# Head norms summed with tokens on partitions, and the state inputs of an S5 layer regrouped

## The reference, cut to what matters

```
x = concat(meta_tokens, x); h = rms_norm(x, norm_pre[0])
q, k, v, gate_a, u, gate_b = split(h @ w_in)          # 8 query heads, 2 key heads of 128
q = rope(rms_norm(q per head, q_norm)); k = rope(rms_norm(k per head, k_norm))
y_a = attention(q, k, v) * silu(gate_a)
# S5, in each of two directions, 64 groups of 16 channels, 64 complex states each:
bu = einsum('blgp,gnp->blgn', u, b_bar); s_t = a_bar * s_(t-1) + bu_t
y_b = glu(gelu(u * d_skip + sum over directions of Re(c . s))) * silu(gate_b)
h = concat(y_a, y_b) @ w_out
```

## Time and profile before

| | us |
|---|---|
| median of 3 runs | 2744.39 |
| lowest, highest | 2741.42, 2744.92 |
| the profiled execution, its own time | 2744.17 |
| its span, first to last instruction | 2742.2 |
| PE busy | 2499.8 (91%) |
| DVE, ACT, POOL busy | 1396.9, 1012.3, 1120.3 |
| mean granted TensorE clock | 0.966 |

### The profile page before, as it was taken

How to read it: one execution, slowest core, us unless ns; L and a number is a source line. 1 busy time by engine, 2 the same in 40 slices (tenths; PEclk the granted TensorE clock), 3 DMA queues, 4 the chain that set the end, 5 groups by cost and what they waited for, 6 DMA issues and landing times. The chain is left out here.

```text
span 2742.2 us, 40562 instructions
## 1 busy us (share of the span) xinstructions
PE 2499.8 (91%) x15206; PEld 2161.4 (79%) x15206; DVE 1396.9 (51%) x2104; ACT 1012.3 (37%) x2146; POOL 1120.3 (41%) x1114
## 2 busy tenths in 40 slices
PE   6999998789998749899799999899898799999798
PEld 6988887678886648777588888787777689999687
DVE  6559886667775125414455443555655442222314
ACT  5232222767664331233233223355565420000331
POOL 3445542077774224411145454443343255554320
PEclk9999999999999979999899999999999899999999
DMA  7424443201103663535424333452434264442544
GB/s 168 111 67 151 140 132 127 99 21 48 48 33 115 155 163 116 174 132 163 117 76 149 129 123 128 149 168 101 165 120 155 74 233 163 140 140 94 189 164 153
DMA packets 271015, 349.27 MB, mean 127 GB/s; under 512 B 45652, under 2 KB 212206, under 8 KB 268406
## 3 DMA queue, kind: packets, MB, share of 16 engines
q1 hardware_dynamic: 226326, 268.32, 31.1%
q10 hardware_dynamic: 44512, 78.53, 8.2%
HBM read 223.23 MB, written 114.03 MB: 123 GB/s over the span
## 5 line engine op out<-in xcount | busy, mean ns | idle before, releaser
L1074 POOL TENSOR_TENSOR w_hi<-w_raw,ones 128x512 fp32r<-128x512 f32 (+1 forms) x232 | 287.3, 1238 | 753.1 <-PE r L1085 326.4
L1085 PE MATMUL r<-h_lo,w_hi 128*128 128x264 f32 (+1 forms) x1200 | 395.2, 329 | 7.4 <-PEq L2508 7.4
L1085 PE MATMUL r<-h_hi,w_lo 128*128 128x264 f32 (+1 forms) x1200 | 386.8, 322 | 0.0
L1085 PE MATMUL r<-h_hi,w_hi 128*128 128x264 f32 (+1 forms) x1200 | 386.0, 322 | 0.0
L1076 POOL TENSOR_TENSOR w_lo<-w_raw,w_hi 128x512 fp32r<-128x512 f32 (+1 forms) x232 | 355.7, 1533 | 18.2
L1085 PEld LDWEIGHTS r<-h_lo,w_hi 128*128 128x128 f32 x1200 | 226.7, 189 | 28.9 <-issue 9.9
L1085 PEld LDWEIGHTS r<-h_hi,w_hi 128*128 128x128 f32 x1200 | 226.8, 189 | 21.3 <-issue 2.4
L1085 PEld LDWEIGHTS r<-h_hi,w_lo 128*128 128x128 f32 x1200 | 226.7, 189 | 17.6
L1813 PE MATMUL o<-v,prob 116*116 116x129 f32 (+1 forms) x1296 | 166.1, 274 | 0.3 <-ACT prob L1863 0.3
L1085 PE MATMUL x<-h_lo,w_hi 128*128 128x264 f32 (+1 forms) x432 | 155.4, 360 | 7.0 <-POOL w_lo L1076 7.0
L1813 PEld LDWEIGHTS o<-v,prob 116*116 116x116 f32 (+1 forms) x1296 | 158.4, 180 | 3.9 <-ACT prob L1863 0.5
(11 more groups left out here) (383 smaller groups left out, 6294.2 us busy)
## 6 DMA issues: line engine op xcount, KB each, us to landing
w_raw<-in_w_in_even SPq DMA_DIRECT2D x72, 256.0 KB, 3.4
w_raw<-in_w_in_odd SPq DMA_DIRECT2D x64, 256.0 KB, 3.5
w_raw<-in_w_ogate SPq DMA_DIRECT2D x64, 256.0 KB, 2.8
v_d<-vs ACTq DMA_DIRECT2D x8, 1152.0 KB, 4.2
us<-u_d SPq DMA_DIRECT2D x16, 520.0 KB, 4.9
xc_d<-xc ACTq DMA_DIRECT2D x8, 1040.0 KB, 6.3
qk_d<-qk ACTq DMA_DIRECT2D x16, 520.0 KB, 2.7
qk<-qk_d SPq DMA_DIRECT2D x8, 1040.0 KB, 5.0
```

The costliest lines, as they stand in the source:

```text
L1074: self.nc.gpsimd.tensor_tensor(hi, raw, one, ALU.mult).then_inc(self.hi_done, 1)
L1085: ins = self.nc.tensor.matmul(bank[:, 0:n], w[:, u % self.buffers, k, :], z[:, off:off + n], start=(first and k == 0 and w is self.hi and ...
```

## The change

1. **Norm sums in front.** For each of the ten norms PE no longer multiplies ones (as weights) with `sq`. It takes slices of `sq` of 104 tokens as weights and one column of ones as the moving operand: ten matmuls, after step 2, each giving 104 sums in one PSUM column. ACT takes one root of 104x10, DVE one reciprocal of 104x10 (`inv`). PE then spreads them again, by ten transposes of a column of `inv` broadcast to 128, four after step 8, four after step 10, two after step 20. DVE multiplies `resn` with them in three parts, straight from PSUM. PE now waits for DVE's reciprocal (`found`) before step 9, and for the first of the three products (`scaled_by`) before the last two transposes. `turn_values` moves from steps 2, 4, 6 to 4, 6, 8.
2. **Six tables given.** `EARLY` goes from 2 to 6: 28 half tables are built after the gates of front instead of 20, and 12 of them are input tables. In s5_states SP loads six tables, for groups 0, 1, 2, 4, 5 and 7; DVE builds those of 3 and 6 there.
3. **State inputs.** The transposes are placed so that the real and imaginary part of one direction lie side by side as 128 weight columns; one matmul makes both. `w_in` has two buffers, and the transposes of group n + 1 go ahead of the sums of group n. The sums go to three PSUM slots of 1024 columns, each with one direction of four channel groups. ACT copies the forward direction to `Z`, DVE the backward one, each with 64 partitions by 4x130.

The diff, cut to its core:

```
-EARLY = 2
+EARLY = 6
...
+    NB, QUAD, SLOTS = G // GB, GB // 2, 3
+    MADE = [n for n in range(NB) if n not in STATES_GIVEN]
...
+            return t["Z"][side * NS:(side + 1) * NS, 1:CH + 1, q, g0:g0 + QUAD].rearrange("p c (b k) -> p b k c", b=2)
+
+        def sums(x, q):
+            return zb[x % SLOTS][q * NS:(q + 1) * NS, :].rearrange("p (b m) -> p b m", b=2)[:, :, 0:2 * CH].rearrange(
+                "p b (k c) -> p b k c", k=2)
+
...
+                        if i >= 2:
+                            sp.wait_ge(turned, 4 * (STATES_GIVEN[i - 2] + 1))
+                        sp.dma_start(given[:, i % 2].rearrange("p q g s f -> p (q g s f)"),
+                                     d["tab_in"][i].rearrange("p q h x -> p (q h x)")).then_inc(tab_loaded[i % 2], 16)
...
+                for n in range(NB):
+                    for h in range(2):
+                        r = 2 * n + h
+                        x = 4 * n + 2 * h + 1
+                        if r < 10:
+                            for k in range(0 if r == 0 else r + 2, r + 3):
+                                table_step(k // 6, k % 6)
+                        dve.wait_ge(summed, x + 1)
+                        for q in range(2):
+                            ins = v.tensor_copy(states(1, q, n, h), sums(x, q))
+                        ins.then_inc(back_out, 1)
...
-                        copied.wait(pe, nb, m - 1)
-                        for n in range(4):
...
-                    for g in range(GB):
-                        stored.wait(pe, nb, g - 3)
-                        for q in range(2):
-                            cols = slice(q * CH, (q + 1) * CH)
-                            nc.tensor.matmul(zp[g % 4][f, cols], wl[:, g, q, f], us[:, nb * GB + g, :],
-                                             start=True, stop=True)
-                            last = nc.tensor.matmul(zp[g % 4][r, cols], wl[:, g, q, r], us[:, nb * GB + g, ::-1],
-                                                    start=True, stop=True)
-                        last.then_inc(summed.sem, 1)
+                        if 4 * n + m >= 2:
...
+                            x = 4 * n + 2 * h + side
+                            if x >= SLOTS:
+                                y = x - SLOTS
+                                pe.wait_ge(back_out if y % 2 else ahead_out, y // 2 + 1)
+                            for k in range(QUAD):
+                                g = QUAD * h + k
+                                u = us[:, n * GB + g, ::-1] if side else us[:, n * GB + g, :]
+                                at = k // 2 * 512 + k % 2 * CH
+                                last = nc.tensor.matmul(zb[x % SLOTS][:, at:at + CH], wl[:, n % 2, g, side, :], u,
+                                                        start=True, stop=True)
+                            last.then_inc(summed, 1)
+
+                turn(0)
+                for n in range(NB):
+                    if n + 1 < NB:
+                        turn(n + 1)
+                    sum_up(n)
...
+                def keep(n):
+                    for m in range(4):
+                        act.wait_ge(turned, 4 * n + m + 1)
+                        if n >= 2:
+                            act.wait_ge(summed, 4 * (n - 1) - (2 if m < 2 else 0))
+                        nc.scalar.activation(wl[:, n % 2, 2 * m:2 * m + 2, :, :].rearrange("p g q m -> p (g q m)"),
+                                             tp[m % 2][:, :], ACT.Copy).then_inc(copied, 1)
+
+                keep(0)
+                for n in range(NB):
+                    if n + 1 < NB:
+                        keep(n + 1)
+                    for h in range(2):
+                        x = 4 * n + 2 * h
+                        act.wait_ge(summed, x + 1)
+                        for q in range(2):
+                            ins = nc.scalar.activation(states(0, q, n, h), sums(x, q), ACT.Copy)
+                        ins.then_inc(ahead_out, 1)
...
+    NORM_COLS, NORM_AT = L // 10, ((0, 4, 0), (4, 8, 1), (8, 10, 0))
...
-                    nc.tensor.matmul(bank[p % 2][:, 0:m], c["ones"][:, :], sq[:, off:off + m],
-                                     start=True, stop=True).then_inc(ss, 1)
...
+                    for i in range(10):
+                        last = nc.tensor.matmul(bank[0][0:NORM_COLS, i:i + 1], sq[:, i * NORM_COLS:(i + 1) * NORM_COLS],
+                                                c["ones"][:, 0:1], start=True, stop=True)
+                    last.then_inc(ss, 1)
...
+                    i0, i1, b = NORM_AT[part]
+                    if part == 0:
+                        pe.wait_ge(found, r + 1)
+                    elif part == 2:
+                        pe.wait_ge(scaled_by, 3 * r + 1)
+                    for i in range(i0, i1):
+                        at = (i - i0) * NORM_COLS
+                        last = nc.tensor.transpose(bank[b][:, at:at + NORM_COLS],
+                                                   inv[0:NORM_COLS, i:i + 1].broadcast_to([NORM_COLS, P]),
+                                                   c["ident"][0:NORM_COLS, 0:NORM_COLS])
+                    last.then_inc(spread, 1)
...
+                        if u - 1 in norm_at and n == 2:
+                            add_squares(norm_at[u - 1])
+                        if u - 1 in norm_at and n in (8, 10, 20):
+                            spread_norms(norm_at[u - 1], (8, 10, 20).index(n))
+                        if u - 1 in value_at and n in VALUE_STEPS:
+                            turn_values(value_at[u - 1], VALUE_STEPS.index(n))
...
+                    if r:
+                        act.wait_ge(spread, 3 * r)
+                    nc.scalar.activation(inv[0:NORM_COLS, :], bank[0][0:NORM_COLS, 0:10], ACT.Sqrt,
+                                         bias=c["eps"][0:NORM_COLS, :], scale=1.0 / HD).then_inc(root, 1)
 
                 def values_out(n, part):
...
+                    dve.wait_ge(root, r + 1)
+                    v.reciprocal(inv[0:NORM_COLS, :], inv[0:NORM_COLS, :]).then_inc(found, 1)
                     do(v.tensor_tensor(resn, qg, rope[:, 0, :], ALU.mult))
-                    for p, (off, m) in enumerate(PIECES):
-                        dve.wait_ge(root, NP * r + p + 1)
-                        ins = v.reciprocal(rs[:, off:off + m], rs[:, off:off + m])
-                        do(ins) if p == NP - 1 else do.free(ins)
                     dve.wait_ge(swapped, 64 * (r + 1))
-                    dve.wait_ge(ss, NP * (r + 1))
                     do(v.tensor_tensor(tm, qs, rope[:, 1, :], ALU.mult))
                     do(v.tensor_tensor(resn, resn, tm, ALU.add))
-                    do(v.tensor_tensor(resn, resn, rs, ALU.mult))
+                    for part, (i0, i1, b) in enumerate(NORM_AT):
+                        cols = slice(i0 * NORM_COLS, i1 * NORM_COLS)
+                        dve.wait_ge(spread, 3 * r + part + 1)
+                        v.tensor_tensor(resn[:, cols], resn[:, cols], bank[b][:, 0:(i1 - i0) * NORM_COLS],
+                                        ALU.mult).then_inc(scaled_by, 1)
+                    dve.wait_ge(scaled_by, 3 * (r + 1))
...
+                    if kind == "in":
+                        m = 2 * STATES_GIVEN[m // 2] + m % 2
```

More of the change, by code:

```diff
@@ L770, in _, with turn @@
             @block.tensor
             def _(pe):
-                turned.start(pe)
-                summed.start(pe)
-                f, r = slice(0, NS), slice(NS, P)
-                for nb in range(G // GB):
-                    b = nb % 2
-                    if nb < EARLY:
-                        pe.wait_ge(tab_loaded, 16 * (nb + 1))
-                    else:
-                        built.wait(pe, nb - EARLY, 1)
+                def turn(n):
+                    if n in MADE:
+                        pe.wait_ge(built, MADE.index(n) + 1)
+                    else:
+                        i = STATES_GIVEN.index(n)
+                        pe.wait_ge(tab_loaded[i % 2], 16 * (i // 2 + 1))
@@ L781, in _ @@
                     for m in range(4):
-                        copied.wait(pe, nb, m - 1)
-                        for n in range(4):
-                            g, q = 2 * m + n // 2, n % 2
-                            last = nc.tensor.transpose(tp[m % 2][:, n * P:(n + 1) * P],
-                                                       table[:, b, q, g].rearrange("p s q -> p (s q)"), c["ident"][:, :])
-                        last.then_inc(turned.sem, 1)
-                    copied.wait(pe, nb, 4)
@@ new lines, in turn, with sum_up @@
+                        for k in range(4):
+                            g, q = 2 * m + k // 2, k % 2
+                            last = nc.tensor.transpose(tp[m % 2][:, k // 2 * 256:k // 2 * 256 + 256].rearrange(
+                                "p (r q m) -> p r q m", r=2, q=2)[:, :, q, :],
+                                                       table(n)[:, q, g].rearrange("p s q -> p (s q)"), c["ident"][:, :])
```

(13 more changed lines are left out.)

126 lines of the change are left out of this document (54 added, 72 removed).

## The result

The changed kernel takes 2757.97 us, the median of five runs, against 2743.93 for the kernel before on the same chip (five runs). The ratio is 1.0045 with a 95% interval of 1.0033 to 1.0058: slower by half a per cent. The profiled execution took 2759.71 us, with a span of 2757.9 against 2742.2, at the same mean clock, 0.966.

The account below looks back on a forecast made before the run. PE was taken to bound front, and ACT in turn with PE s5_states. Front +10 and s5_states -3.5 made +6.5 on 2744.17, 2750.7, given as 2750.8 us since that run was 0.2 below the median; 80% range 2739 to 2760.

Parts of the forecast that it names:

- the forecast's own case: Whole kernel: front +10 and s5_states -3.5 give 2750.8 us, from 2746 to 2755; held at 50%.
- The sign: Whole kernel: slower than 2749.9 us 45%, the same 43%, faster than 2738.9 us 12%.
- s5_states: State inputs stage: 3.5 us shorter, with bounds from 3 us longer to 13 us shorter.
- Front: Norm sums on PE: each norm costs 1.0 us more, ten norms +10 us, bounds +1 to +17.
- Rival (a): Front: weight loads are cheap, 50 to 62 ns a pass, front +1 to +4, total 2741 to 2745; 25%.
- rival (d): Front: weight loads do not overlap at all, 0.11 us or more a pass, front +17, total 2758; 5%.
- DVE in front: Front: 66 us less reciprocals, 45 us more half tables, none on the path; PE's waits for DVE cost nothing.
- rival (c): Front: PE waits for DVE at step 9, 12 us more, 2763, or less of it, 2755 to 2758; 10%.
- The first copies: Start of s5_states: four more weight copies go ahead, so first copies begin at 487.7 instead of 485.81.
- The period: s5_states, per group: 6.6 us against 7.08, with 3.8 for four ACT copies and 0.25 of gap left.
- The end: End of s5_states: DVE's last copies end 1 us after ACT's, at 535.9 against 539.54.
- rival (b): s5_states: half the partitions make ACT's copies cheap, stage gains 13 us, total 2741, or 2733 with cheap loads; 10%.

Follow-up runs that it names:

- experiment 11: The changed kernel with each norm's ten products issued twice; 2788.94 us, ratio 1.0165 to the kernel before.
- Experiment 1: The kernel before with the new norm sums alone, two tables given and the old s5_states; 2754.68 us, ratio 1.0034.
- experiment 3: The kernel before with six tables given (`EARLY = 6`) and nothing else changed; 2755.73 us, ratio 1.0032.
- experiment 2: The kernel before with six tables given and the new s5_states, but the old norm sums; 2760.49 us, ratio 1.0049.
- experiment 4: The changed kernel with state copies written side by side instead of 512 bytes apart (inputs in wrong places); ratio 1.0015 to the kernel before.
- experiment 5: The changed kernel with 128x260 copies alternating on ACT and DVE, 64 column weights, six PSUM slots; 2748.06 us, ratio 1.0011 to the kernel before.
- experiment 9: The kernel before's norm, tables 0, 1, 3, 5 given, 128x260 copies on ACT and DVE; 2746.14 us, ratio 1.0004 to the kernel before.
- experiment 10: The kernel before's norm, tables 0, 1, 3 given, 128x260 copies on ACT and DVE; 2753.51 us, ratio 1.003 to the kernel before.
- experiment 12: The kernel before's norm, tables 0, 2, 4, 6 given, 128x260 copies on ACT and DVE; 2739.94 us, ratio 0.9985 to the kernel before.

## Why the prediction was right or wrong

The median lies 7.2 us over the forecast of 2750.8 and inside the range of 2739 to 2760, but above the 2746 to 2755 of the forecast's own case. None of the four rivals happened. The sign was one that I gave 45%. That the total stayed in the range is in part luck: the upper end was kept for loads that don't overlap and for waits on DVE, neither of which came, and s5_states with +4.3 lies outside the -13 to +3 that I had given it.

**Front, right.** Ten products took 1.87 us (1.8 forecast), four transposes 461.61 - 460.99 less one 512 column step of 0.23, so 0.39 (0.36 forecast), a norm 1.07 more (1.0 forecast). The slope of weight loads over columns was the right row, and the transposes at 62 ns the wrong one. Rival (a) is ruled out by these rows and by experiment 11, rival (d) too. Experiment 1 has the term by itself: 10.2 us.

**DVE in front, right, for a reason only half seen.** PE shows no wait for DVE, as forecast, so rival (c) did not happen. The root is found early enough: DVE's timeline of the kernel after at the same norm, with its last table step, the short reciprocal and the swap's arrival, answers to the earlier trace rows:

```profile
456.95 0.69 DVE L718 TENSOR_TENSOR staged<-staged 128x512 f32<-128x512 f32 x1
458.99 0.22 DVE L1682 RECIPROCAL inv_norm<-inv_norm 104x10 f32<-104x10 f32 x1 [1.35 <-ACT inv_norm L1464]
...
464.00 1.24 DVE L1685 TENSOR_TENSOR work<-work,scratch 128x1040 f32<-128x1040 f32 x1 [3.70 <-DMA work<-work]
```

DVE has done the second half table 1.35 us before it is needed, and PE asks for the reciprocal only at 460.99. What I did not see is that the eight further half tables are free only because the 6.68 us of reciprocals are gone (experiment 3).

**s5_states, wrong: -3.5 forecast, +4.3 measured.** The miss of 7.8 us, term by term, each counted from the memset:

- *The first copies*, forecast 11.8 us after the start, came at 502.51 - 488.45 = 14.06: 2.3 late. 1.3 is the later landing of the first table (open). The rest is that PE turns two groups before the first sums: 24 transposes run from 494.53 for 5.71 us, 0.24 each, where the clock is 0.50 until some 500 us, and I had priced the second group's weight copies by ACT's own time.
- *The period*, 6.6 forecast, was 7.04 to 7.11, and 7.87 where a table made by DVE was late (0.85 in place of 0.25 in the row of 514.76; twice). Six periods took 44.03 us instead of 39.6: 4.4. Of that 1.6 is the late tables. The other 2.8 is the price of a copy: I took 0.95 us for 520 elements, from 1.77 ns an element in the earlier trace rows, and it was 1.07. Those rows have copies that overlap: eight of 0.64 us each in 3.89. Four of 1.06 in 4.35 do not overlap at all, and neither do DVE's (two of 1.05 in 2.11). I had taken the overlap over into copies of another shape, which no row supported.
- *The end.* The forecast let DVE's last copies end 1 us behind ACT's, 8.6 us after the last two groups began; it took 9.8, since the copies are 1.07 and DVE starts one later: 1.2.

The sum is 2.3 + 4.4 + 1.2 = 7.9.

Not all of the +4.3 is the price of the new stage. The old stage, its code unchanged, took 64.2 us in the kernel before but 66.2 and 66.3 in experiments 1 and 3, where the clock came back 13.5 and 14.3 us after the memset instead of 8. In the kernel after it came back after 11.7 us, in experiment 2 after 9.1, and there the same new stage took 66.6. Kernel against kernel with only the stage's code changed, or with the tables that belong to it, the new stage costs 0.3 us (experiments 3 and 2) to 2.3 (experiment 1 and the kernel after). The forecast started from a profile in which the clock came back early, and put what a later return costs at nothing. The times alone don't part the new stage from the old one: the intervals of experiment 1 and of the whole change overlap. What doesn't depend on the start is the period, 7.04 to 7.13 us in both kernels with the new stage (from ACT's first copy to its last 51.8 and 51.9 us) against 6.6 forecast.

The mechanism that I gave, that ACT's time goes by far written elements and that 64 partitions help nothing, was right: experiments 4 and 5 rule out rival (b). The Trainium skill (SBUF — State Buffer, the note on cachelines in the section "Door 1: The DMA port swizzle") speaks of a penalty for each new line without naming an engine. The runs agree with it for both: 463 ns more per 520 far elements on ACT, 352 on DVE. The second miss was to call DVE "at most as long as ACT" by its total. Its copies and table steps stand in one queue, and a table can be late while DVE's sum is in balance; it stood idle for 19.3 us before its copies, 11.4 of them at the start, and still its tables were late twice. Experiments 9, 10 and 12 show how much hangs on that.

**The rest.** 12.5 + 4.3 = 16.8 us, of which the later stages give back 1.1: the span grew by 15.7. (What follows the stage took between 2194.9 and 2205.4 us in the profiles of these kernels, so the 1.1 says nothing.) The profiled run was the slowest of its five, that of before an average one; the medians differ by 14.0, which is 10.7 for the norms and 4.3 for the states, less 1 that I can't place. So of my forecast of +6.5 the +10 held, and of the -3.5 nothing was seen: between +0.3 and +4.3 came in its place.

## What to carry over

Where an operation costs by the far elements that one partition writes, as here, moving data to a second engine helps only if each engine then writes fewer elements per partition: halve those, not the partitions. A product with one moving column is not small; it costs its weight loads, 94 ns each with 104 columns when nothing longer stands beside them. And when an idle engine is given work in another engine's queue of needs, look at when each result is wanted, not only at the sum of busy times: with the same four tables, giving every second one made the kernel faster than before, and two other choices did not. And before a stage's length from one profile is taken as the base of a forecast, look at where the clock stood in it: here that alone was worth 2 us.

## What the runs showed of the hardware

- A copy's time went by the elements of a partition and by the distance of its writes, not by the number of partitions. Near writes on ACT: 64x520 takes 600 ns, 128x512 takes 596 (experiment 4 and the kernel after). Writes 512 bytes apart, f32: 64x520 takes 1063 ns on ACT and 1050 on DVE, where near ones take 600 and 698; 128x260 takes 638 and 622 (experiment 12). I had expected a difference between ACT and DVE.
- Successive copies of one engine overlapped with 128 partitions and did not with 64: two weight copies of 128x512 with 0.60 us each take 1.09 on ACT, but two near copies of 64x520 with 0.60 each take 1.21 (experiment 4, ACT's timeline), and two far ones on DVE 2.11 at 1.05 each. Whether the partitions or the shape decide this was not tried apart.
- 3.6 us of weight loads with one moving column each were followed by some 3 us at half the granted clock behind seven of ten norms, although PE counts as busy throughout; 1.87 us of them were not. It cost 1.2 us a norm on the average, beside the 1.8 of the added loads (experiment 11).
- At the start of s5_states PE has been idle for 12 to 15 us. The clock was back at 1.00 about 8, 13.5 and 14 us after the memset, and the same code of the stage took 64.2, 66.2 and 66.3 us (the kernel before, experiments 1 and 3). Why it comes back at different times was not tried.
